# Work moved from VectorE to ScalarE, and taps, norms and a state recurrence moved between units, in the projection passes of a four-mixer decoder layer

## What is computed

```python
h = rmsnorm(x, norm_g)
z = jnp.einsum('btd,de->bte', h, w_in)
q_a, k_att, v_a, f_a, g_a, sh_b, g_b, u_c, g_c, u_d, g_d = split_cols(z)
# B: RWKV-7
xm = sh + rw_mu * (prev - sh)                  # prev: the row one token earlier
r, k, v, wd, ad = jnp.split(xm, RWKV_SPLITS, axis=-1)
kk = kk * lax.rsqrt(jnp.maximum(jnp.sum(kk * kk, axis=-1, keepdims=True), 1e-12))
s_final, o = lax.scan(rwkv7_step, s0, xs)      # prompt, and 4 steps for the samples
# D: convolution module
glu = u1 * jax.nn.sigmoid(u2)
y = depthwise_conv(concat([buf, glu]), conv_w) + conv_b   # width 31
yn = (y - mean) * lax.rsqrt(var + LN_EPS) * ln_g + ln_b
out = jax.nn.silu(yn) @ pw_out                 # later times silu(g_d)
```

## Time and profile before

| | |
|---|---|
| median of 3 runs | 1674.64 us (1670.19 to 1675.73) |
| profiled execution, its own time | 1666.86 us |
| its span, first to last instruction | 1665.1 us |
| TensorE matmul busy | 1553.4 us (93%) |
| VectorE busy | 987.7 us (59%) |
| ScalarE busy | 602.8 us (36%) |
| GpSimd busy | 82.1 us (5%) |
| mean granted TensorE clock | 0.976 of full |

### The profile page before, as it was taken

The page is one execution under the profiler, slowest core; times in us unless marked ns, Lnnn a source line. Parts: engine busy times, 40 slices in busy tenths (PEclk is TensorE's granted clock), DMA queues, the critical chain, the costliest instruction groups (busy, mean ns, idle before and its releaser), DMA issues.

```text
span 1665.1 us, 35933 instructions
## 1 busy us (share of the span) xinstructions
PE 1553.4 (93%) x14428; PEld 1152.3 (69%) x14428; DVE 987.7 (59%) x2382; ACT 602.8 (36%) x1235; POOL 82.1 (5%) x97
## 2 busy tenths in 40 slices
PE   7979999999999999997777999998999999999998
PEld 5867778888887888886644666667887865444443
DVE  5689764767457666678375666634554549333333
ACT  3234342443434441334444565543333353010001
POOL 1010000000000000000000000000000003222220
PEclk9999999999999999999879999999999999999999
DMA  6354473446544374344758746668575559999983
GB/s 225 116 189 160 163 280 129 154 142 235 198 134 158 111 262 143 112 159 157 237 197 241 198 142 187 176 202 245 170 220 177 185 197 357 358 337 353 354 314 132
DMA packets 184495, 341.71 MB, mean 205 GB/s; under 512 B 22213, under 2 KB 124101, under 8 KB 173638
## 3 DMA queue, kind: packets, MB, share of 16 engines
q1 hardware_dynamic: 167338, 256.88, 47.3%
q0 software_dynamic: 10496, 72.98, 11.7%
q10 hardware_dynamic: 6496, 9.56, 1.5%
HBM read 286.13 MB, written 55.35 MB: 205 GB/s over the span
## 4 chain that ended last, share of the span: by engine, by line
PE 45%; ACT 3%; DMA 2%; issue 1%; DVE 1%; SPq 1%; ACTq 0%; DVEq 0%
PE psum L1323 24%; PE psum L1017 5%; PE psum L1269 4%; PE psum L1197 4%; PE psum L1283 4%; PE psum L1628 2%; PE psum L1044 1%; PE psum L1531 1%; DMA big<-lfD 1%; DMA big<-zT 1%; ACT big L1712 1%; PE psum L1031 1%; SPq L817 0%; DMA big<-rkv 0%; ACT big L1964 0%
## 5 line engine op out<-in xcount | busy, mean ns | idle before, releaser
L1044 PE MATMUL psum<-big 128*128 128x256 f32 (+1 forms) x1920 | 438.7, 386 | 11.2 <-DVE big L2085 9.3
L1044 PEld LDWEIGHTS psum<-big 128*128 128x128 f32 x1920 | 367.3, 192 | 70.4 <-DVE big L2085 10.1
L1725 ACT ACTIVATE zst<-psum 128x256 f32<-128x256 f32 (+1 forms) x336 | 126.7, 384 | 442.5 <-PE psum L1044 440.5
L1323 PE MATMUL psum<-big 64*64 64x64 f32 (+4 forms) x5440 | 256.1, 270 | 16.0 <-issue 9.3
L1323 PEld LDWEIGHTS psum<-big 64*64 64x64 f32 (+2 forms) x5440 | 176.8, 131 | 100.8 <-issue 74.7
L1044 PE MATMUL psum<-big,wbuf 128*128 128x256 f32 (+1 forms) x768 | 181.3, 384 | 0.0
L1044 PEld LDWEIGHTS psum<-big,wbuf 128*128 128x128 f32 x768 | 146.2, 191 | 23.0 <-issue 0.4
L2269 DVE SCALAR_TENSOR_TENSOR big<-big,pars 128x512 f32<-128x512 f32 x240 | 161.0, 744 | 0.4
L979 POOL DMA_INDIRECT big<-in_cache_v,pidx x64 | 68.2, 1065 | 687.3 <-PE psum L1283 474.1
L1197 PE MATMUL psum<-big 64*128 64x512 f32 (+3 forms) x320 | 74.9, 578 | 18.4 <-DMA big<-zT 12.3
L1712 ACT ACTIVATE big<-big 128x512 f32<-128x512 f32 (+11 forms) x108 | 83.9, 803 | 11.2 <-DVE big L2345 7.5
(11 more groups left out here) (322 smaller groups left out, 2028.7 us busy)
## 6 DMA issues: line engine op xcount, KB each, us to landing
big<-in_k_pages SPq DMA_DIRECT2D x432, 128.0 KB, 2.3
big<-wS SPq DMA_DIRECT2D x36, 768.0 KB, 5.8
zst<-in_k_pages SPq DMA_DIRECT2D x80, 128.0 KB, 2.7
wS<-big SPq DMA_DIRECT2D x12, 768.0 KB, 5.7
wbuf<-in_w_pairs SPq DMA_DIRECT2D x18, 512.0 KB, 3.9
big<-in_w_pairs SPq DMA_DIRECT2D x18, 512.0 KB, 4.4
zT<-big ACTq DMA_DIRECT2D x16, 512.0 KB, 3.4
rwS<-big SPq DMA_DIRECT2D x32, 256.0 KB, 3.6
```

The lines of the kernel that those rows point to most:

```text
L1044: last = nc.tensor.matmul(psum[:, bank, 0:wide(p) // 2], left(k), right(k), start=first and k == 0, stop=k == 3, skip_group_check=True)
L1323: return nc.tensor.matmul(out, l, r, start=start, stop=stop, skip_group_check=True)
L1725: nc.scalar.activation(parts_[:, U % 2, COPIED_TO[j], 0:n], psum[:, (0, 1, 2, 0, 1, 2, 3)[j], 0:n], ACT.Copy, scale=0.125 if i == U_QA els ...
```

## The change

It does the following.

- ScalarE multiplies the next pass's x rows by norm_g, one row of 512 between the copies of each of units 2 to 9; VectorE's `normed` is then two products with the inverse root.
- The key floor goes to ScalarE (`key_sums`: Relu of the sum less 1e-12, and the logarithm adds 1e-12 again), at the start of unit 6.
- For r, k and v ScalarE makes the previous token's row times mu (`shifted`, in units 4, 5 and 6, after the second copy), VectorE then only row times (1 - mu) plus that (`mix_pair`). That pair now stands behind the unit's taps. The scratch for it is `sig_w`, so the lora's gates wait for the mixing of v.
- The sigmoid of `u2d` goes before the second copy of unit 3; `lora_inputs` goes from unit 3 to unit 5.
- Copies of the samples' states go to ScalarE, at the start and in unit 11 of pass 0.
- `sample_taps` goes to unit 1 of pass 1; with it the samples' columns of mean, variance and output of the convolution go from pass 0 to pass 1, and their gate is kept in `gate_ds`.
- The recurrence's steps go to units 0 to 2 of pass 3, its last output to unit 3.
- `TAPS` has no taps at unit 8 any more; mean and variance stand at units 8 and 10 in every pass, pass 3 too; `conv_norm` stands before unit 11's sums, `conv_root` and `conv_silu` of pass 3 inside unit 11.
- SyncE loads the value weights before it stores the second half of the scan rows; `pool_sums` waits for those stores.

```diff
-        TAPS = ((0, 0, 5, 4, 4, 4, 6, 8, 0), (0, 0, 5, 4, 4, 4, 6, 8, 0), (0, 0, 5, 4, 4, 4, 6, 8, 0), (0, 0, 1, 1, 5, 5, 6, 7, 6))
+        TAPS = ((0, 0, 4, 4, 4, 4, 7, 8), (0, 0, 4, 5, 5, 5, 6, 6), (0, 0, 4, 5, 5, 5, 6, 6), (0, 0, 1, 5, 6, 7, 6, 6))
...
-        MEAN_AT, VAR_AT = (8, 8, 8, 9), (10, 10, 10, 11)
+        MEAN_AT, VAR_AT = 8, 10
...
                     if i == 10:
-                        store_scan_rows(p, 1)
                         if p + 1 < PASSES:
                             sp.wait_ge(pool_stored, stores(p))
                             wvf_load(p + 1, 1)
+                        store_scan_rows(p, 1)
...
+            def key_sums(p):
+                for t in TILES:
+                    for h in HALVES:
+                        a_(kinv[:, t, half(p, h)], of_small(('key', p, t, h))[:, 0:wide(p) // 2], ACT.Relu, sr_act, bias=under)
+
+            def shifted(p, i):
+                act.wait_ge(z_add, adds_through(p, i))
+                act.wait_ge(halo_in, 3 * p + i - U_R + 1)
+                for r in range(2):
+                    a_(sig_w[:, r, 0:PT_W], ek[:, EK_ROWS[i - U_R] + r, 0:PT_W], ACT.Copy, mu_ready, scale=par7[:, 8 + 2 * (i - U_R) + r:9 + 2 * (i - U_R) + r])
...
             def lora_gates(p):
+                act.wait_ge(sh_done, mixed_through(p, MIX_V))
...
             def unit(p, i):
-                copies(p, i, 0, 2)
+                if i == 6:
+                    key_sums(p)
+                copies(p, i, 0, 1)
+                if i == 3:
+                    gate(p, U_U2, ACT.Sigmoid, u2d)
+                copies(p, i, 1, 2)
...
-                if i == 3:
-                    lora_inputs(p)
+                if i in (4, 5, 6):
+                    shifted(p, i - 1)
                 copies(p, i, 2, 3)
...
-                if i == 3:
-                    gate(p, U_U2, ACT.Sigmoid, u2d)
+                if i == 5:
+                    lora_inputs(p)
...
                 copies(p, i, 5, 6)
+                if 2 <= i < 2 + KT and p + 1 < PASSES:
+                    row = hb[(p + 1) % 2][:, i - 2, 0:PT_W]
+                    a_(row, row, ACT.Copy, gained, scale=par7[:, i - 2:i - 1])
...
+                dve.wait_ge(gained, KT * p)
                 for h in HALVES:
-                    for k in range(KT):
-                        row = hb[p % 2][:, k, half(p, h)]
-                        ins = v.scalar_tensor_tensor(row, row, par7[:, k:k + 1], rs[h], ALU.mult, ALU.mult)
-                        ch.mark(ins)
+                    row = hb[p % 2][:, :, half(p, h)]
+                    ch.mark(v.tensor_tensor(row, row, rs[h].unsqueeze(1).to_broadcast([P, KT, PT_W // 2]), ALU.mult))
...
             def mix_pair(p, i):
-                mix(p, 2 * (i - U_R), 2, sig_w[:, :, 0:PT_W])
+                at, n = EK_ROWS[i - U_R], 2 * (i - U_R)
+                dve.wait_ge(mu_ready, 2 * (3 * p + i - U_R + 1))
+                for r in range(2):
+                    row = ek[:, at + r, 1:1 + PT_W]
+                    v.scalar_tensor_tensor(row, row, one_m_mu[:, n + r:n + r + 1], sig_w[:, r, 0:PT_W], ALU.mult, ALU.add).then_inc(sh_done, 1)
...
                 for i in range(UNITS):
-                    if i == 6:
-                        key_norms(p)
...
+                    if i == 11:
+                        conv_norm(p)
                     evac(p, i)
...
                     if i == 1:
+                        if p == 1:
+                            sample_taps(0)
+                            sample_taps(1)
...
                     if i in (3, 4, 5):
-                        mix_pair(p, i)
-                    if i == 3 and p == 0:
-                        sample_taps(0)
-                        sample_taps(1)
+                        mix_kept(p, i)
...
-                    if 2 <= i <= 8:
+                    if 2 <= i <= 7:
                         taps_at(p, i)
-                    if i == 8 and MEAN_AT[p] == 8:
+                    if i in (3, 4, 5):
+                        mix_pair(p, i)
+                    if i == 8:
                         centered(p)
```

218 lines of the change are left out of this document (122 added, 96 removed).

## The result

The changed kernel took 1654.2 us (median of 4 runs, 1647.25 to 1656.89), the kernel before 1672.4 us over all its runs of the comparison (4, 1664.34 to 1675.73). The ratio is 0.9892, 95% interval 0.9855 to 0.9928: 18.2 us faster, where 24.8 were forecast. The range of 1638 to 1662 us held it, but the forecast gain is a ratio of 0.9852, just outside the interval, so the change most likely gave less than its sum. The profiled execution took 1656.43 us (span 1654.5), only 10.4 us less than the one of before: it is at the upper end of its runs, that of before near the lower end of its own.

The account below looks back on a forecast made before the run. TensorE, busy 1553 of 1665 us, bounds the kernel; only its idle stretches or clock can give time. -9.5 - 4.4 - 1.3 - 1.3 - 8.3 = -24.8 us: 1674.64 becomes 1649.8 us, range 1638 to 1662.

Parts of the forecast that it names:

- Pass 0, -9.5: Units 3 to 9 of pass 0: both pair-sum waits and their slow clock go, small new waits come; -9.5 us.
- the value weights, -4.4: Start of pass 1: value weights load ahead of scan-row stores, so the 2.88 us wait and 1.5 us slow clock go.
- The key wait of 1.1 us: End of unit 5, passes 1 and 2: TensorE waits 1.1 us for key squares, since mixing stands behind the taps.
- Passes 1 and 2, -1.3 each: Each pass: mean's wait falls from 2.92 to 0.5 us, less a new 1.1 us key wait; gain 1.3 us.
- Pass 3, -8.3: Pass 3: mean's wait and its clock go (-11.9 us); key 0.6, mean 1.3, variance 1.7 us come; -8.3 us.
- Its step then ends at about 691 us with TensorE needing it at 694: nothing, 3 us of slack: Pass 3, samples' recurrence one unit earlier: the step with the second row load costs TensorE nothing, 3 us of slack.
- After 831 us nothing changes but the start.: Stages behind the projections: they only start earlier and add no gain or loss, 0 us.
- (b): Rival: key and mean waits bring three more clock drops at 1.8 us, ScalarE's price 0.76; +6.5, 1656 us; chance 0.2.
- (a): Rival: two clock drops at the lora gates vanish, perhaps the key waits too; 1643.5 us; chance 0.2.
- (c): Rival: in unit 5, mixing products behind the taps become the bound, 8 us four times; +7, 1682 us; chance 0.04.
- (d): Rival: ScalarE's added copies and floors, 35 us, delay the copies products wait for; +10, 1685 us; chance 0.03.
- (e): Rival: no change, removed waits come back one unit later, VectorE nearly full in units 3 to 9; 1674 us; chance 0.07.

Follow-up runs that it names:

- again: Changed kernel, no edit, profiled a second time (that execution 1646.98 us); timed 1648.54 us, ratio 0.9873 to the kernel before.
- mean_late: Changed kernel with pass 3's mean back in unit 9 behind `pool_gated`, variance in unit 11, root, norm and silu behind the last product: 1654.94 us, ratio 0.9909.
- after: First profile of the changed kernel, no edit against it: profiled execution 1656.43 us, span 1654.5 us.
- no_sample_taps: Kernel before the change with the samples' convolution left out, a copy of the gated values in its place: 1665.32 us, ratio 0.9964.

## Why the prediction was right, and where it was off

- **Pass 0, -9.5, and the value weights, -4.4.** Together -13.9, measured -13.7 and -13.0. Up to the first value product of pass 1, without its wait, it is -9.8 in both profiles, and the wait with its clock gave -3.9 and -3.2. Both waits for pair sums are gone. The order of the weights, tested alone, is 4.2 us. Their wait did not vanish, it is 0.5 to 1.3 us in the profiles with the new order. The mean was to wait 0.7 us more than 2.11, and waits 2.63; the lora gates were to wait 0.2 us more than 0.77, and wait 1.45. Which of the parts pulled the pair sums forward was only half right: the samples' taps by themselves are 3.5 us, and the subtractions were not needed for it, since with them back no pair sum waited. The earlier GLU, the tap less in unit 2 and the key floors have no run of their own, so their shares are open.
- **The key wait of 1.1 us.** 0.96 and 0.96 in passes 1 and 2, 0.8 (forecast 0.6) in pass 3, at the place and by the chain that the prediction gave: in "again" the mixing ends at 316.4, the key squares start at 316.42, the key sums at 317.86.
- **Passes 1 and 2, -1.3 each.** The mean's wait fell from 2.92 to 0.7 (forecast 0.5), the lora wait grew from 1.20 to 1.47 us, which the prediction had not. Pass 2 gained 0.5, pass 1 1.0 or 2.4 us, and the 1.4 us between the two are the clock behind the lora wait. Its "stays with its 1.8 us of clock" is right 13 times in 24 in these two passes. The Trainium skill (TensorE: Matmul & The Clock Gate, "What's actually happening") names 1.2 GHz the default that activity lifts; the rows agree in so far as the low level follows waits, and show that one and the same wait may or may not bring it.
- **Pass 3, -8.3: the step that failed.** -2.4 and -5.0 measured. The 11.9 us went, and mean_late shows that the bank held the mean. Against it came the terms foreseen (key 0.8, mean 1.1, variance 1.7; together the 3.6 us of the forecast) and two that were put at nothing. "Its step then ends at about 691 us with TensorE needing it at 694: nothing, 3 us of slack": the need was right, the step was not. In after TensorE asked at 679.8 us, which is 694.5 counted as in the profile of before, and the step ended at 681.5, which is 696.2. Its row landed 11.4 us after the weights of the next unit were first issued, at the end of unit 2, where some 5 us had been taken. TensorE waited 1.75 and 0.89 us, with 1.7 us of clock in after. And in pass 3 the clock was high behind the lora wait in the profile of before, low in both of after (1.7 us), and that wait is 0.3 us longer; the prediction had no term for either. From "again": -11.9 + 0.8 + 1.1 + 1.7 + 0.9 + 0.3 + 1.7 = -5.4, measured -5.0.
- **"After 831 us nothing changes but the start."** So in the work, not in the time. The first scores start 15 us behind the last product, 14 before, in every profile with the variance ahead of it and the load in its place (14.7 to 15.3). The traces give a likely reason: in unit 11 of pass 3 ScalarE's store of gated values (512 KB) now stands behind the root of the variance. It is issued 0.1 us after the last product, together with SyncE's loads, and takes 8.3 to 9.3 us where SyncE's loads are in their place; in before, mean_late and no_sample_taps it is issued 1.7 us ahead of the last product, lands in 2.8 us, and the scores start 14.0 to 14.5 us behind it. No run moves that store alone. The rest varied from 547 to 555 us behind the first rwkv matmuls over all 14 profiles, whose code is the same there.
- **The rivals.** (b), new drops, is nearest: 1656 us against 1654.2, but it is the state step and the lora gates that brought them, not the key sums and means. (a) came in part in "again", where the drop in pass 1 stayed away; that is luck, by the 6 of 12 above. (c) did not come: 1 us, not 8. (d) was right in kind: the row copies cost 0.7 us in each of passes 1 and 2 and 0.5 us in pass 0. The Trainium skill (ScalarE: Activation LUTs, "Rules for kernel authors") would keep these multiplications on VectorE. For the row copies the runs agree, by these 0.7 us; for the mixing they show that moving it gained nothing, since VectorE had room for it. The page's own reason is the speed per element, which no run here tests. The price was 0.7 us for a row with a scale, where I took 0.6. (e) is out by the interval.

## What to carry to other kernels

Before work is moved off a busy engine, look at whether it idles ahead of the step that others wait for: only what stands behind its last input counts there, and moving taps out of the last unit did what moving 15 us of mixing to ScalarE did not. A wait of TensorE in the middle of a step costs its length and here, by luck, 1.7 us of slow clock; so compare stages, landmark to landmark, over several profiles, and do not read a difference of 5 us between two spans. And when a chain gets shorter, ask what it now allows: the change had finished the convolution 8 us before the scores, and only the order on TensorE kept 7 us of that from the time.

## What was not expected of the hardware

The same wait of 1.46 us, in the same place and in kernels that are the same up to the few edits above, was followed by a granted clock at the lower of its two levels (1.2 of 2.4 GHz) for some 3.5 us in some executions and not in others: 23 of 36, and most often in pass 3. With no wait but the usual, 200 us of rwkv matmuls ran at 1.00 in one profile and at 0.97 to 0.98 in another, which is 5 us. With 1 MB of decay rows issued right ahead of the 1 MB of the first keys, the keys landed 6.1 us later than with the rows behind them, and the rows 3.0 us earlier; the later of the two landed 14.9 us behind the last product in one order and 14.3 us in the other, so the pair together gained 0.6 us.
